# One change to the scan stage of a two-block network on one core: the order of a group's chunk products, step sizes in the exponent, features copied by ScalarE, and where the transfers are issued

## The reference, cut to what matters

```
xbc = silu(causal_depthwise_conv(xbc, conv_w, conv_b))      # 24 tiles of 128 channels: B 4, C 4, x 16
dt = softplus(dt_raw + dt_bias);  a = -exp(a_log)
x_ = xs * dt                                                # per head and token
a_cum = cumsum(dt * a)                                      # within each chunk
scores = C . B ;  decay_in[l, s] = exp(a_cum[l] - a_cum[s]) for l >= s
y_diag = (scores * decay_in) x_
chunk_states = B . (exp(a_cum[end] - a_cum) * x_)
state = state * exp(a_cum[end]) + chunk_states              # carried from chunk to chunk
y_off = (C . state) * exp(a_cum)
y = (y_diag + y_off + xs * d_skip) * silu(z), then a norm for each group
```

## Time and profile before

| | |
|---|---|
| median of 3 runs | 1637.16 us (1635.53 to 1640.14) |
| the profiled execution | 1638.42 us, its span 1636.6 us |
| TensorE products busy | 1615.0 us, 99% of the span |
| VectorE / ScalarE / GpSimd busy | 64% / 45% / 41% |
| convolution (tiles 0 to 23 on TensorE) | about 532 to 664 us of the span |
| scan with z | about 664 to 840 us |

### The profile page before, as it was taken

One profiled execution on the slowest core, in us unless ns is written; L12 is line 12 of the kernel. 1 busy time (PEld: TensorE's weight loads), 2 busy tenths in 40 slices (PEclk: granted clock), 3 DMA queues, 4 the chain that ended last, 5 costly groups with the idle time before them and its releaser, 6 DMA issues.

```text
span 1636.6 us, 22469 instructions
## 1 busy us (share of the span) xinstructions
PE 1615.0 (99%) x7955; PEld 1279.3 (78%) x7955; DVE 1048.2 (64%) x1672; ACT 733.8 (45%) x1274; POOL 663.8 (41%) x307
## 2 busy tenths in 40 slices
PE   7999999999999999999999999999999999999999
PEld 6688777777888888777778877777788888888887
DVE  6599686677336877777775077876766765665100
ACT  5433365565345645544553244444524444343210
POOL 4244564323454344344464332222144354444442
PEclk9999999999999999999999999999999999999999
DMA  6233321214333244211113321111233233233331
GB/s 210 65 118 101 91 78 54 75 52 141 91 103 103 65 135 131 70 52 52 52 60 96 90 73 57 52 54 50 87 118 99 77 103 103 90 103 92 101 96 59
DMA packets 40408, 143.25 MB, mean 88 GB/s; under 512 B 4729, under 2 KB 5209, under 8 KB 39937
## 3 DMA queue, kind: packets, MB, share of 16 engines
q1 hardware_dynamic: 37600, 131.96, 26.5%
q10 hardware_dynamic: 2720, 10.11, 1.7%
HBM read 137.57 MB, written 4.48 MB: 87 GB/s over the span
## 4 chain that ended last, share of the span: by engine, by line
PE 49%; DVE 1%; ACT 1%; issue 0%; ACTq 0%; DVEq 0%
PE bank L767 10%; PE bank L769 9%; PE bank L768 9%; PE bank L1420 4%; PE bank L1419 4%; PE bank L1421 4%; PE bank L1305 2%; PE bank L1326 1%; PE bank L1314 1%; PE bank L1273 1%; PE bank L1281 0%; ACT w_hi L1441 0%; ACT gm L1981 0%; PE bank L788 0%; PE bank L789 0%
## 5 line engine op out<-in xcount | busy, mean ns | idle before, releaser
L632 POOL TENSOR_TENSOR w_lo<-w_raw,w_hi 128x1024 fp32r<-128x1024 f32 x243 | 597.5, 2462 | 938.0 <-ACT w_hi L1441 800.5
L767 PE MATMUL bank<-u_hi,w_hi 128*128 128x512 f32 x776 | 332.0, 428 | 1.4 <-ACT gm L1981 0.8
L769 PE MATMUL bank<-u_hi,w_lo 128*128 128x512 f32 x776 | 305.3, 393 | 0.0
L768 PE MATMUL bank<-u_lo,w_hi 128*128 128x512 f32 x776 | 304.7, 393 | 0.0
L1441 ACT ACTIVATE w_hi<-w_raw 128x1024 fp32r<-128x1024 f32 x199 | 209.4, 1056 | 210.3 <-PE bank L769 169.7
L767 PEld LDWEIGHTS bank<-u_hi,w_hi 128*128 128x128 f32 x776 | 146.7, 189 | 43.4 <-issue 11.4
L768 PEld LDWEIGHTS bank<-u_lo,w_hi 128*128 128x128 f32 x776 | 147.1, 190 | 32.8 <-issue 4.6
L769 PEld LDWEIGHTS bank<-u_hi,w_lo 128*128 128x128 f32 x776 | 146.8, 189 | 32.3
L1419 PE MATMUL bank<-u_hi,w_hi 128*128 128x512 f32 x288 | 112.0, 389 | 0.0
L1420 PE MATMUL bank<-u_lo,w_hi 128*128 128x512 f32 x288 | 112.0, 389 | 0.0
L1421 PE MATMUL bank<-u_hi,w_lo 128*128 128x512 f32 x288 | 112.0, 389 | 0.0
(11 more groups left out here) (476 smaller groups left out, 3436.9 us busy)
## 6 DMA issues: line engine op xcount, KB each, us to landing
w_raw<-weights SPq DMA_DIRECT2D x243, 512.0 KB, 3.6
xt<-x_t SPq DMA_DIRECT2D x8, 256.0 KB, 6.6
hank<-bias_dram ACTq DMA_DIRECT2D x8, 256.0 KB, 4.0
xt<-x_t ACTq DMA_DIRECT2D x1, 2048.0 KB, 8.4
h_dram<-h_res ACTq DMA_DIRECT2D x1, 2048.0 KB, 7.7
h_res<-h_dram ACTq DMA_DIRECT2D x1, 2048.0 KB, 7.5
out<-h_res SPq DMA_DIRECT2D x8, 256.0 KB
p_val<-p_t ACTq DMA_DIRECT2D x1, 512.0 KB, 10.6
```

The lines of the kernel that those rows point to most:

```text
L632: pool.tensor_tensor(w_lo[:, j, :], w_raw[:, j, :], w_hi[:, j, :].bitcast(F32), ALU.subtract).then_inc(w_lo_ready, 1)
L767: pe.matmul(o, hi, xh, start=(i == 0), stop=False)
L768: pe.matmul(o, hi, xl, start=False, stop=False)
L769: mm = pe.matmul(o, lo, xh, start=False, stop=(i == n - 1))
```

## The change

- **Chunk products in a row.** `chunk_state(g, 0)` and `(g, 1)`, from group 1 on also `(g, 2)`, are issued ahead of the next pair's `spread_keys` and `spread_features`, with no z parts between them. The two z parts come after.
- **Step sizes as logarithms.** r_dt is clamped at 1e-37, ScalarE takes its logarithm in iteration 1, and VectorE subtracts a_cum. This log(dt) − a_cum is the bias of the key exponentials, so that the weights hold dt themselves, and r_dte is the exponential of it plus a_cum at the chunk's end. `cols` holds two kinds in place of three, with 8 transposes for 12, and the four negations go.
- **Features copied by ScalarE.** xdt is replaced by x_tok, a plain copy out of PSUM by ScalarE (`feature_tokens`). VectorE makes only the three xdec, from PSUM, after the copy.
- **Rows in three partitions.** stack_a goes to DRAM and comes back as a_rows: for each head its three bf16 parts on three adjacent partitions, at 32 times (h mod 4). `spread_keys` issues both masks first, then a product with a 3-row slice of ones for each head; `spread_features` uses the same slices.
- **Transfers one to a tile.** one_hot and tri_b are gone; stack_a is stored at i = 13, trig is loaded at i = 14, and the four parts of a_rows at i = 16 to 19. TensorE's `spread_keys(0)` waits for all four.

```diff
-            pe.wait_ge(consts2_in, 16 * 3)
-            pe.wait_ge(cols_ready, 3)
-            pe.wait_ge(stack_a_ready, 1)
+            pe.wait_ge(rows_in, 16 * 4)
+            pe.wait_ge(cols_ready, 2)
             spread_keys(0)
...
             def spread_keys(p):
 
+                if p:
+                    pe.wait_ge(l_ready, 2 * p)
+                for s in range(2):
+                    pe.matmul(bank[4 + s][:, :], ident_b[:, :], later4_b[:, :], start=True, stop=False)
                 for h in (2 * p, 2 * p + 1):
-                    if p:
-                        pe.wait_ge(l_ready, h - 1)
-                    o = bank[4 + h % 2][:, :]
-                    pe.matmul(o, one_hot[:, h:h + 1].broadcast_to([96, P]), stack_a[:, :], start=True, stop=False)
-                    pe.matmul(o, ident_b[:, :], later4_b[:, :], start=False, stop=True).then_inc(a_spread, 1)
+                    k = slice(32 * (h % 4), 32 * (h % 4) + 3)
+                    pe.matmul(bank[4 + h % 2][:, :], ones_b[k, :], a_rows[k, h // 4, :], start=False,
+                              stop=True).then_inc(a_spread, 1)
...
-                    r = slice(64 * (h % 2), 64 * (h % 2) + 64)
-                    mm = pe.matmul(bank[2][r, :], one_hot[:, h:h + 1].broadcast_to([96, SSD_P]), stack_a[:, :],
-                                   start=True, stop=True)
+                    r, k = slice(64 * (h % 2), 64 * (h % 2) + 64), slice(32 * (h % 4), 32 * (h % 4) + 3)
+                    mm = pe.matmul(bank[2][r, :], ones_b[k, 0:SSD_P], a_rows[k, h // 4, :], start=True, stop=True)
...
+                chunk_state(g, 0)
+                chunk_state(g, 1)
+                if g:
+                    chunk_state(g, 2)
                 spread_keys(4 * g + 1)
                 spread_features(4 * g + 1)
-                chunk_state(g, 0)
-                column_tile(z, of_u2, part=(6, 7))
-                chunk_state(g, 1)
-                column_tile(z, of_u2, part=(7, 8))
-                chunk_state(g, 2)
+                if not g:
+                    chunk_state(g, 2)
+                column_tile(z, of_u2, part=(6, 8))
...
-                for dst, name in ((one_hot, "one_hot"), (trig, "trig"), (tri_b, "tri_b")):
-                    act.dma_start(dst[:, :], a[name]).then_inc(consts2_in, 16)
+
+            def load_rows(q):
+
+                act.wait_ge(h_spilled, 16 * 3)
+                src = bass.AP(a_dram.tensor, q * S, [[32 * S, 3], [4 * S, SSD_H // 4], [1, S]])
+                act.dma_start(a_rows[32 * q:32 * q + 3, :, :], src).then_inc(rows_in, 16)
...
+            def feature_tokens(g, c):
+
+                act.wait_ge(x_turned, NT * g + c + 1)
+                act.copy(x_tok[:, c, :], bank[group_bank(g, c)][:, :]).then_inc(x_tok_ready, 1)
...
                 if i == 12:
                     send_residual()
+                if i == 13:
+                    act.wait_ge(stack_a_ready, 1)
+                    act.dma_start(a_dram, stack_a[:, :]).then_inc(h_spilled, 16)
+                if i == 14:
+                    act.dma_start(trig[:, :], a["trig"]).then_inc(consts2_in, 16)
+                if 16 <= i < 20:
+                    load_rows(i - 16)
+                if i == 1:
+                    act.wait_ge(steps_ready, 1)
+                    act.activation(r_dt[:, :], r_dt[:, :], ACT.Ln).then_inc(dt_log, 1)
...
+                dve.tensor_scalar(r_dt[:, :], r_dt[:, :], 1e-37, None, ALU.max).then_inc(steps_ready, 1)
...
-                dve.sem_inc(acum_ready, 1)
+                dve.memset(ones_b[:, :], 1.0).then_inc(ends_ready, 1)
+                dve.wait_ge(dt_log, 2)
+                link(dve.tensor_tensor(r_dt[:, :], r_dt[:, :], r_ac[:, :], ALU.subtract))
+                dve.sem_inc(steps_ready, 1)
...
-                for c in range(NT):
-                    n = NT * g + c
-                    dve.wait_ge(x_turned, n + 1)
-                    x3 = xdt[:, c, :].rearrange("p (h f) -> p h f", f=SSD_P)
-                    dve.tensor_tensor(x3, bank[group_bank(g, c)][:, :].rearrange("p (h f) -> p h f", f=SSD_P),
-                                      spread_col(3 * c, 8 * g, 8), ALU.mult).then_inc(xdt_ready, 1)
-                    if c < 3:
-                        dve.wait_ge(xdt_ready, n + 1)
-                        dve.tensor_tensor(xdec[:, c, :].rearrange("p (h f) -> p h f", f=SSD_P), x3,
-                                          spread_col(3 * c + 1, 8 * g, 8), ALU.mult).then_inc(xdec_ready, 1)
+                for c in range(3):
+
+                    dve.wait_ge(x_tok_ready, NT * g + c + 1)
+                    dve.tensor_tensor(xdec[:, c, :].rearrange("p (h f) -> p h f", f=SSD_P),
+                                      bank[group_bank(g, c)][:, :].rearrange("p (h f) -> p h f", f=SSD_P),
+                                      spread_col(2 * c, 8 * g, 8), ALU.mult).then_inc(xdec_ready, 1)
```

More of the change, by code:

```diff
@@ L417, in build @@
         stored = sem("stored")
-        tri_b = at("tri_b", 55.5, [P, P], BF16)
         y = at("y", 104, [P, 16, S])
         y_lo = at("y_lo", 104, [P, 16, S], F32R)
-        one_hot = at("one_hot", 206.5, [96, SSD_H], BF16)
+        ones_b = at("ones_b", 206.5, [P, P], BF16)
+        a_rows = at("a_rows", 56, [P, SSD_H // 4, S], BF16)
+        a_dram = nc.dram_tensor("a_dram", (96, S), BF16).ap()
         trig = at("trig", 148, [P, S])
@@ L441, in build @@
         scores = at("scores", 178.5, [P, S])
-        xdt = at("xdt", 180.5, [P, NT, S])
+        x_tok = at("x_tok", 180.5, [P, NT, S])
         xdec = at("xdec", 188.5, [P, 3, S])
@@ L548, in build @@
         x_turned = sem("x_turned")
-        xdt_ready = sem("xdt_ready")
+        x_tok_ready = sem("x_tok_ready")
+        rows_in = sem("rows_in")
         xdec_ready = sem("xdec_ready")
@@ L1057, in _ @@
                 if t is st["ssd_c"][2]:
-                    pe.wait_ge(acum_ready, 1)
-                    pe.wait_ge(ends_ready, 1)
+                    pe.wait_ge(steps_ready, 2)
+                    pe.wait_ge(ends_ready, 2)
                     pe.wait_ge(norm_std, 3)
@@ L1068, in _ @@
             for c in range(NT):
-                for i, r in enumerate((r_dt, r_dte, r_ac)):
-                    k = SSD_H * (3 * c + i)
+                for i, r in enumerate((r_dte, r_dt)):
+                    k = SSD_H * (2 * c + i)
                     mm = pe.transpose(bank[5][:, k:k + SSD_H], r[:, c * P:(c + 1) * P], ident[0:SSD_H, 0:SSD_H])
@@ L1123, in turn_x @@
                 if c == 3:
-                    pe.wait_ge(xdt_ready, NT * g + 1)
+                    pe.wait_ge(x_tok_ready, NT * g + 1)
+                    pe.wait_ge(xdec_ready, 3 * g + 1)
                 o = bank[group_bank(g, c)]
@@ L1207, in _ @@
                             r, f = slice(64 * (h % 2), 64 * (h % 2) + 64), (h % 8) * SSD_P
-                            mm = pe.matmul(bank[6][r, c * P:(c + 1) * P], xdt[:, c, f:f + SSD_P],
+                            mm = pe.matmul(bank[6][r, c * P:(c + 1) * P], x_tok[:, c, f:f + SSD_P],
                                            weight(h)[:, c * P:(c + 1) * P], start=True, stop=True)
@@ L1888, in _ @@
                 if g:
-                    group_out(g)
+                    act.wait_ge(y_dot, 8 * g)
+                else:
+                    act.wait_ge(conv_ready, len(conv_tiles))
+                for c in range(NT):
+                    if g and c == 1:
+                        group_out(g)
+                    feature_tokens(g, c)
                 act.wait_ge(state_dot, 3 * g + 1)
@@ L2002, in _ @@
             query_squares(0)
-            act.wait_ge(krope_ready, 1)
+            act.wait_ge(latent_consts, 1)
             key_squares(0)
-            act.wait_ge(half_ready, 2)
+            act.wait_ge(latent_consts, 3)
             key_features(0)
@@ L2012, in _ @@
             values_out(1)
-            act.wait_ge(half_ready, 1)
+            act.wait_ge(latent_consts, 2)
             head_probs(0)
@@ L2800, in _ @@
             b0 = VEC["gate_b"][0]
-            dve.tensor_scalar(half_b[:, :], vecs[:, b0:b0 + XH], 0.5, None, ALU.mult).then_inc(half_ready, 1)
+            dve.tensor_scalar(half_b[:, :], vecs[:, b0:b0 + XH], 0.5, None, ALU.mult).then_inc(latent_consts, 1)
             for r in (0, 64):
@@ L2806, in _ @@
             link(ins)
-            dve.sem_inc(half_ready, 1)
+            dve.sem_inc(latent_consts, 1)
             for x in (q_s, k_s):
```

31 lines of the change are left out of this document (13 added, 18 removed).

## The result

The changed kernel has a median of 1641.49 us (1639.05 to 1644.48, 20 runs), the kernel before, run beside it, 1638.38 us (1635.49 to 1640.46, 20 runs). The ratio is 1.0021 (95% interval 1.0015 to 1.0027): about 3.1 us or 0.21% slower, clear of the noise of the runs but within the 0.3% set for no change, and at the forecast time (1641.4, range 1637.0 to 1646.5). The hit is better than the forecast: that one was a rise of 4.2 us on a base of 1637.16 from three runs. The profiled execution took 1643.28 us, its span is 1641.5.

What follows compares the result with a forecast made beforehand. TensorE, busy for 99% of the span, was taken as the bound. The terms −4.0 + 1.0 + 5.6 + 1.65 = +4.2 us raised the median from 1637.2 to 1641.4 us, range 1637.0 to 1646.5.

Steps and rivals of the forecast that it cites:

- Part 1: Scan, chunk products in a row: all four TensorE stops for chunk states go, 4 x 0.99 = 4.0 us gained.
- Part 2: Scan, key and feature rows: three-partition products run side by side but pay for tile shape switches, +1.0 us.
- Part 3: Before the first key rows near 640 us: TensorE waits for the fourth load of rows, 5.6 us lost (4.3 to 8.1).
- Part 4: Behind the stop for the rows: TensorE's clock runs at its lower level for a stretch, +1.65 us (0 to 3.3).
- it hangs on when GpSimd's subtraction meets VectorE, which may shift either way: Scan, the existing 0.7 us TensorE wait for weight_b: said to stay, with no term in the sum.
- behind its taps and behind a weight split: ScalarE's iteration 19: the fourth load of rows is issued only after both, at 643.5 us.
- With nothing in front: Fourth load of rows: issue and landing priced at 2.1 us, from a 256 KB transfer with no other ahead.
- rival B: After the stop for the rows: the clock stays at 2.4 GHz; +2.6 us, median 1639.7, chance 0.22.
- The stall isn't given back: Stop for the rows near 640 us: its time stays lost, since TensorE is the bound afterwards as well.
- D: Rows transfer lands late or ScalarE isn't earlier at tile 19: stop 8.1 instead of 5.6 us, 1643.9, chance 0.10.
- E: Scan: state stops survive because ScalarE copies or VectorE come over 1.2 us late; +4.0 us, 1645.4, chance 0.03.
- F: Scan rows: narrow shape switches are free and all row products overlap; −5.1 instead of +1.0 us, chance 0.05.

Runs made afterwards that it cites:

- old_order: Changed kernel with the earlier order of chunk products, key rows and z parts put back; median 1643.51 us, ratio 1.0030 to the kernel before the change.
- order_alone: Kernel before the change with only the new order of chunk products; median 1636.04 us, ratio 0.9990 to the kernel before.
- one_hot_again: Changed kernel with stack_a and one_hot used as before instead of the three-partition rows, new mask order kept; median 1633.06 us, ratio 0.9968 to the kernel before.
- one_row_group: Changed kernel with both heads of a pair in the same three partitions; median 1643.51 us, ratio 1.0035 to the kernel before.
- last_load_gap: Changed kernel with the fourth a_rows load issued at the end of iteration 18, after VectorE's end of tile 18; median 1636.59 us, ratio 1.0000 to before.
- busy_wait: Changed kernel with 22 mask products put before TensorE's wait for the rows, their result overwritten; median 1639.44 us, ratio 1.0006 to the kernel before.
- rows_pairs: Changed kernel with the four a_rows loads issued two each in iterations 16 and 17; median 1634.60 us, ratio 0.9978 to the kernel before.

## Why the prediction was right, by its own steps

| term | forecast | measured |
|---|---|---|
| Part 1, stops for states | −4.0 | −3.8, and a new stop of +0.85 in group 0 (old_order) |
| Part 2, key and feature rows | +1.0 | −0.3 to 0 |
| Part 3, stop for the rows | +5.6 | +4.95 |
| Part 4, clock | +1.65 | +2.2 to 2.3 |
| fewer transposes | "tenths" | −0.3 |
| sum at the scan's end | +4.2 | +3.7 |

The mechanisms held, but that 1641.4 met 1641.49 so closely is luck. Part 3 was 0.65 us too long and Part 4 as much too short; Part 1 left out a stop of 0.85, and Part 2 was at least 1.0 too dear. And the rise was put on a median of three runs, 1637.16, where twenty give 1638.38.

**Part 1** held in mechanism and size. In group 1 the products now stand in a row and VectorE's state instructions follow them:

```profile
718.05 2.74 PE L1139 MATMUL bank<-xdec,b_tok 128*128 128x512 f32 x6
720.62 0.59 PE L1080 MATMUL bank<-squares_b 128*128 128x512 bf16 x2
...
723.39 1.09 PE L1212 MATMUL bank<-weight_a,x_tok 128*64 128x128 f32 x16
724.41 0.94 PE L1218 MATMUL bank<-c_t,states 128*128 128x128 f32 x6
```

```profile
719.97 3.35 DVE L2685 SCALAR_TENSOR_TENSOR states<-states,chunk_decay,bank 128x64 f32<-128x64 f32 x16 [0.85 <-PE bank L1139]
```

VectorE ends at 723.32 and TensorE wants the states at 724.41, 1.1 us of slack where I had worked out 1.2, and the weighted products run into the state products in 1.02 us instead of the 1.96 of the earlier trace rows. old_order gives the 3.8 us of the four stops back, 2.98 net of group 0. The sentence "it hangs on when GpSimd's subtraction meets VectorE, which may shift either way" was left at nothing in the sum, and it shifted for the worse. In group 0 of after:

```profile
687.29 2.40 POOL L633 TENSOR_TENSOR w_lo<-w_raw,w_hi 128x1024 fp32r<-128x1024 f32 x1 [11.83 <-ACT w_hi L1445]
```

```profile
688.28 1.83 DVE L2701 TENSOR_TENSOR y<-y,e_ac 128x384 f32<-128x384 f32 x1
```

```profile
692.19 1.09 PE L1212 MATMUL bank<-weight_b,x_tok 128*64 128x128 f32 x16 [0.80 <-DVE weight_b L2667]
```

VectorE's addition takes 1.83 us, where its neighbour of the same shape takes 0.56, while GpSimd's subtraction runs; the weight behind it is 0.80 us late. In old_order that subtraction ends at 689.66, the addition begins at 690.21 and takes 0.56, and group 0 has no stop for weight_b. In order_alone, one_hot_again and one_row_group the two meet again (1.83 or 1.84 us), and the stop is there. So the order causes the stop, and the meeting goes with it; no run moved GpSimd's subtraction alone.

**Part 2** had the right mechanism (side by side, with a price for the switch) and a size that was too large. A pair takes 1.17 us from its first mask to the weighted products (815.28 to 816.45) where I gave 1.27 to 1.35, and 1.20 before. The keys with the switch behind them take 0.32, where the sum had 0.21 + 0.2: between two of the narrow shapes the switch costs about 0.1, by my estimate from these rows. one_hot_again puts the gain of the narrow rows at 0.3 us or less, and old_order's scan is 0.3 us shorter than that of before.

**Part 3** came near by two errors that cancel. ScalarE's timeline after, iteration 12 and iteration 19 (beside the earlier trace rows), and the pieces of the chain that ended last around the load (start, us, what):

```profile
609.86 0.63 ACT L1886 ACTIVATE taps_sg<-taps 128x512 f32<-128x512 f32 x1 [0.90 <-ACT r_out L1804]
...
640.74 0.78 ACT L1855 ACTIVATE taps<-bank,vecs 128x512 f32<-128x512 f32 x1 [2.61 <-DVE y L2630]
640.85 0.70 ACTq L1813 DMA_DIRECT2D a_rows<-a_dram  x1
641.42 1.04 ACT L1445 ACTIVATE w_hi<-w_raw 128x1024 fp32r<-128x1024 f32 x1
```

```profile
639.02 1.64 DVE y L2630
...
640.85 3.93 DMA a_rows<-a_dram
```

First, the issue was 2.65 us earlier than forecast (640.85, not 643.5). The saving of iteration 12 was as forecast (−2.6), but the delay of the early part was 0.4 us instead of 1.6 (the taps of iteration 12 begin at 606.76 after and at 606.36 before), so the taps of tile 19 begin at 640.74 and not at 641.9. And the step that failed is "behind its taps and behind a weight split". Both stand ahead of the load in ScalarE's list, but the DMA is issued 0.11 us after the taps begin, and 0.57 before the split begins. The taps waited last for VectorE's multiplication, done at 640.66, and not for tile 19, whose last product had ended at 640.04.

Second, the landing took 3.9 us and not 2.1. SyncE had issued a weight chunk at 640.27. The queues of the DMA engines in 642.4 to 642.9, and below in 643.4 to 643.9 (q1 SyncE's, q10 ScalarE's; packets, MB, share of the 16 engines):

```profile
q1 hardware_dynamic: 52, 0.20, 99.6%
```

```profile
q10 hardware_dynamic: 27, 0.02, 14.1%
```

The chunk fills the engines until 642.9 and thins out up to 643.4. The rows' 27 packets run after it, all of them within half a microsecond, and the landing is seen at 644.79. The Trainium skill ("DMA: Bandwidth & Descriptors", "Why a DMA increments its semaphore by 16 and not by 1") says that such a transfer is spread over the largest number of DMA engines, up to 16, that divides its slowest dimension, here 3. The trace agrees: 27 packets are 3 times 8 of 1 KB and one more. last_load_gap prices the parts: 2.8 us with no chunk ahead, so 1.2 for it. "With nothing in front" was the wrong row for this place, and my bound of 3.6 was under the measured landing too.

**Part 4** had the right mechanism, and rival B is out. The term was mis-sized: 2.2 to 2.3 us in after, not 1.65, and 3.1 in old_order, still inside the bound of 3.3. It is not set by the length of the stop alone. busy_wait shows it as a thing of its own. Stop and clock together are 7.24 us, and the forecast had 7.25: there the two errors cancel.

**The rest.** "The stall isn't given back" held: rows_pairs, which removes it, gets all 7.2 us at the scan's end. Of the other rivals, D was half true: the transfer landed 1.8 us later than forecast, but ScalarE was so much earlier that the stop came out shorter. E did not happen, and F's premise (free switches) was only half true.

## What to carry to other kernels

A load whose issuer waits for the same tile that its consumer follows, or for something later, cannot be hidden, however short it is: put its issue some tiles earlier (here two loads each in iterations 16 and 17, 7.2 us for a moved line), and price it by what is in the DMA engines then, not by its bytes. The price of a stop of TensorE is its length plus what the clock takes afterwards, so work without a use in the wait buys back the second part. That second part varies from one execution to the next: read from one profile, it would be charged to whatever else the kernel changes, so compare stretches that leave it out. When an order change removes a wait, look at who waits next for the engine that was late: here the products themselves (2.1 us with the order alone), and a weight 0.8 us late in another group.

## What the hardware showed that I had not expected

- A DMA in ScalarE's list was issued 0.11 us after the activation ahead of it began, and 0.57 us before the next one ahead of it began (640.85, 640.74 and 641.42), so it did not wait for either to end.
- A load of 24 KB on 3 partitions took 2.8 us from issue to use with nothing ahead (last_load_gap), and 4.0 us with a weight chunk of 512 KB issued in another queue 0.6 us before it (after).
- Stops of 4.8 to 5.0 us brought TensorE's clock to the 1.2 GHz level for 6.8 us in three profiles. It fell between 2.9 us (after) and 5.3 us (one_row_group) from the beginning of the stop, and so cost 2.2 us in after and 3.1 in old_order. Stops of 0.70, 0.80 and 1.90 us cost nothing beyond their length.
- Two bf16 products of 3 rows and 512 columns in different partitions take 0.32 us together with the switch behind them, and 0.53 us in the same ones.
- In the same attention code the clock falls to 1.2 GHz two to five times in the ten profiles, while TensorE is busy, and each time goes with about 1.6 us: the span behind the scan varies by 4.8 us in kernels that are equal there. What decides how often it falls stays open.
